# TensorE's program behind the experts put on both sides of the branch, and the compressed keys' product turned round and fed from split weight units

## What is computed

```python
chunks = kv.reshape(2, B, n_chunk, CMP_STRIDE, G, Dh)      # 16 tokens each
w1r = w1.reshape(2, r, CMP_STRIDE, Dh, CMP_HIDDEN)         # 2 x 2048 x 128 in all
pre = b1
for j in range(r):                                          # r = 2
    part = einsum('kbnpgd,kpdh->kbngh', chunks + pe, w1r[:, j])
    pre = pre + part[:, :, j:j + n_cmp]                     # n_cmp = 15
return einsum('kbcgh,khd->kbcgd', silu(pre), w2) + b2
```

## Time and profile before

| | us |
|---|---|
| median of 3 runs (lowest, highest) | 1060.5 (1059.07, 1060.95) |
| the profiled execution's own time | 1060.7 |
| span of its profile (first to last instruction) | 1058.7 |
| PE busy / PEld busy | 1012.6 / 844.4 |
| DVE busy / ACT busy | 734.1 / 609.1 |
| mean granted TensorE clock | 0.985 of full |

### The profile page before, as it was taken

How to read it: one execution, slowest core, us unless ns; L and a number is a source line. 1 busy time by engine, 2 the same in 40 slices (tenths; PEclk the granted TensorE clock), 3 DMA queues, 4 the chain that set the end, 5 groups by cost and what they waited for, 6 DMA issues and landing times.

```text
span 1058.7 us, 13638 instructions
## 1 busy us (share of the span) xinstructions
PE 1012.6 (96%) x5237; PEld 844.4 (80%) x5237; DVE 734.1 (69%) x813; ACT 609.1 (58%) x694; POOL 51.7 (5%) x47
## 2 busy tenths in 40 slices
PE   7999999997899999999799999999998898999998
PEld 6788788787788888877578888897877687888887
DVE  5534885678999999999955556566487755555664
ACT  6476433538899999988743443345375345344331
POOL 0011561011000000000000000000000000000000
PEclk9999999997999999999999999999899999999999
DMA  8923444452999999999946555873420044555511
GB/s 297 336 83 120 134 145 150 148 186 85 320 373 386 387 386 386 386 386 387 346 145 202 195 191 167 281 271 126 157 80 2 1 159 164 197 194 193 174 70 40
DMA packets 117021, 223.29 MB, mean 211 GB/s; under 512 B 6426, under 2 KB 12713, under 8 KB 116970
## 3 DMA queue, kind: packets, MB, share of 16 engines
q1 hardware_dynamic: 116426, 221.08, 60.2%
q0 software_dynamic: 384, 1.24, 0.3%
q10 hardware_dynamic: 160, 0.27, 0.1%
HBM read 221.49 MB, written 1.07 MB: 210 GB/s over the span
## 4 chain that ended last, share of the span: by engine, by line
PE 79%; DVE 8%; DMA 7%; ACT 4%; issue 2%; DVEq 0%; ACTq 0%; SPq 0%
PE ps L1830 18%; PE ps L1832 18%; PE ps L1831 18%; DMA w_raw<-in_w_exp_gate 6%; PE ps L2127 5%; PE ps L2128 5%; DVE w_lo L965 3%; ACT w_hi L537 2%; PE ps L2151 2%; PE ps L2168 1%; PE ps L2381 1%; PE ps L1996 1%; DMA w_raw<-in_w_exp_down 1%; PE ps L1876 1%; PE ps L1825 1%
## 5 line engine op out<-in xcount | busy, mean ns | idle before, releaser
L965 DVE TENSOR_TENSOR w_lo<-w_raw,w_hi 128x2048 fp32r<-128x2048 f32 x204 | 464.7, 2289 | 144.3 <-ACT w_hi L537 140.6
L537 ACT ACTIVATE w_hi<-w_raw 128x2048 fp32r<-128x2048 f32 x204 | 390.9, 1917 | 215.8 <-PE ps L1832 199.5
L1830 PE MATMUL ps<-w_hi,h_hi 128*128 128x512 f32 (+1 forms) x704 | 273.6, 389 | 9.7 <-DVE h_lo L992 6.7
L1831 PE MATMUL ps<-w_lo,h_hi 128*128 128x512 f32 (+1 forms) x704 | 268.8, 382 | 0.0
L1832 PE MATMUL ps<-w_hi,h_lo 128*128 128x512 f32 (+1 forms) x704 | 268.7, 382 | 0.0
L1830 PEld LDWEIGHTS ps<-w_hi,h_hi 128*128 128x128 f32 x704 | 133.3, 189 | 38.0 <-issue 11.7
L1832 PEld LDWEIGHTS ps<-w_hi,h_lo 128*128 128x128 f32 x704 | 133.2, 189 | 26.0
L1831 PEld LDWEIGHTS ps<-w_lo,h_hi 128*128 128x128 f32 x704 | 133.4, 189 | 23.8
L1830 PE MATMUL ps<-w_hi,aT_hi 128*128 128x512 f32 x176 | 68.9, 391 | 0.0
L1832 PE MATMUL ps<-w_hi,aT_lo 128*128 128x512 f32 x176 | 68.5, 389 | 0.0
L1831 PE MATMUL ps<-w_lo,aT_hi 128*128 128x512 f32 x176 | 68.5, 389 | 0.0
(11 more groups left out here) (354 smaller groups left out, 1276.3 us busy)
## 6 DMA issues: line engine op xcount, KB each, us to landing
w_raw<-in_ffn_w_in SPq DMA_DIRECT2D x44, 1024.0 KB, 5.1
w_raw<-in_w_exp_gate SPq DMA_DIRECT2D x32, 1024.0 KB, 10.7
w_raw<-in_w_exp_up SPq DMA_DIRECT2D x32, 1024.0 KB, 9.8
w_raw<-in_w_exp_down SPq DMA_DIRECT2D x32, 1024.0 KB, 10.8
w_raw<-in_w_in SPq DMA_DIRECT2D x22, 1024.0 KB, 7.8
w_raw<-in_ffn_w_out SPq DMA_DIRECT2D x22, 1024.0 KB, 5.0
w_raw<-in_w_mix_in SPq DMA_DIRECT2D x8, 1024.0 KB, 6.3
w_raw<-in_w_out SPq DMA_DIRECT2D x4, 1024.0 KB, 5.0
```

Source lines behind the costliest of these rows:

```text
L537: act.activation(w_hi[:, u % SPLIT, :], w_raw[:, u % RAW, :], ACT.Copy).then_inc(hi_ready, 1)
L965: dve.tensor_tensor(w_lo[:, u % SPLIT, :], w_raw[:, u % RAW, :], w_hi[:, u % SPLIT, :], ALU.subtract).then_inc(lo_ready, 1)
L1830: pe.matmul(out, hi, w_h, start=first, stop=False)
L1831: pe.matmul(out, hi, w_l, start=False, stop=False)
```

## The change

PE's program behind the experts becomes a function that is written once on each side of the branch (so on the few side no jump lies between the experts and the first FFN). The compression takes its weights from two more units of the common ring (8 of the 16 steps each, keys and values side by side), and the roles are turned: the columns of activations, hi and lo packed to 128, are the stationary side, and 256 weight columns move, once from `w_hi` and once from `w_lo`. A small product with `fold` sums the hi and lo rows. ACT and DVE make the packed hi and lo parts; the splits are reordered around the two new units. POOL loses one memset.

```diff
-U_MIXOUT = U_MIX + 8
+U_MIXOUT = U_MIX + 10
+U_CMP = (U_MIX + 5, U_MIX + 7)
+        kv_cmp = region_r("kv_cmp", 4096, PAIRS, 2, 2, 32)
+        def u_mix(i, kh):
+            return U_MIX + (0, 1, 2, 3, 4, 6, 8, 9)[2 * i + kh]
-        cmp_w1 = region(4096, 2, PAIRS, P)
-        kvT = region(13824, 2, 3, S)
+        cmp_sums = region(6144, 2, P)
+        def kv_src(g, odd):
+            v = ps[g * DH:(g + 1) * DH, 4, :].rearrange("p (k s) -> p k s", k=2)
+            return bass.AP(v.tensor, v.offset + odd, [list(v.ap[0]), list(v.ap[1]), [CMP_STRIDE, N_CMP], [2, PAIRS]])
+        def kv_of(low, g, odd):
+            v = kv_cmp[odd * DH:(odd + 1) * DH, :, low, :, N_CMP * g:N_CMP * (g + 1)]
+            return v.rearrange("p pp k c -> p k c pp")
...
 # SP
-            sp.dma_start(cmp_w1, a["cmp_w1_2"][0].rearrange("k (pp q) h -> q k pp h", q=P)).then_inc(cmp_in, 16)
-            for j in range(8):
-                mix_load(U_MIX + j)
+            def cmp_load(half):
+                u = U_CMP[half]
+                sp.wait_ge(lo_ready, u - RAW + 1)
+                dst = w_raw[:, u % RAW, :].rearrange("p (pp k h) -> p pp k h", k=2, h=P)
+                for kv, landed in enumerate((raw_in[u % RAW], cmp_in)):
+                    sp.dma_start(dst[:, :, kv], a["cmp_w1_2"][0, kv].rearrange(...)[:, 8 * half:8 * half + 8]).then_inc(landed, 16)
+            (mix_load of the units in order, cmp_load(0) behind (2, 0), cmp_load(1) behind (2, 1))
...
 # ACT
             leave_mix(0)
             split_hi(U_MIX + 4)
-            split_hi(U_MIX + 5)
+            act.wait_ge(cmp_in, 48)
+            split_hi(U_CMP[0])
+            act.wait_ge(kv_T, 1)
+            for g in range(2):
+                for odd in range(2):
+                    act.activation(kv_of(0, g, odd), kv_src(g, odd), ACT.Copy).then_inc(kv_hi, 1)
             leave_mix(1)
             split_hi(U_MIX + 6)
             head_rms(0, 16, 2)
-            split_hi(U_MIX + 7)
             act.wait_ge(gates_T, 2)
             (two sigmoids of the gates)
+            split_hi(U_CMP[1])
+            split_hi(U_MIX + 8)
+            leave_mix(2)
+            split_hi(U_MIX + 9)
             act.wait_ge(bias2_set, 1)
             (two silus to hidT)
-            leave_mix(2)
-            split_hi(U_MIX + 8)
+            split_hi(U_MIXOUT)
             head_rms(16, 24, 3)
-            split_hi(U_MIX + 9)
+            split_hi(U_MIXOUT + 1)
...
 # DVE
             sum_blocks(0)
+            (positions copied to kv_cmp, hi and lo, 4 small instructions)
-            split_lo(U_MIX + 5)
+            split_lo(U_CMP[0])
             dve.wait_ge(kv_T, 1)
             for g in range(2):
-                dve.tensor_copy(kvT[0:DH, :, g, :], src).then_inc(kvT_ready, 1)
-                dve.tensor_copy(kvT[DH:P, :, g, 0:S - 1], src[:, :, 1:S]).then_inc(kvT_ready, 1)
+                dve.wait_ge(kv_hi, 2 * g + 2)
+                for odd in range(2):
+                    dve.tensor_tensor(kv_of(1, g, odd), kv_src(g, odd), kv_of(0, g, odd), ALU.subtract).then_inc(kvT_ready, 1)
...
-            split_lo(U_MIX + 7)
+            split_lo(U_CMP[1])
             (nsink)
+            split_lo(U_MIX + 8)
+            dve.wait_ge(unit_used, U_CMP[1] + 1)
+            dve.tensor_copy(cmp_sums.rearrange("p k h -> p (k h)"), ps[:, 4, 0:2 * P]).then_inc(kvT_ready, 1)
+            sum_blocks(2)
             dve.wait_ge(pre_T, 1)
             (bias2)
-            split_lo(U_MIX + 8)
-            sum_blocks(2)
+            split_lo(U_MIX + 9)
             inv_rms(16, 24, 2)
             scale_keys(0, OFF_KA, 16)
             scale_heads(OFF_QB, 20, 4)
             scale_heads(OFF_QB + 256, 0, 4).then_inc(q_normed, 1)
+            split_lo(U_MIXOUT)
             dve.wait_ge(kvc_ready, 1)
...
-            split_lo(U_MIX + 9)
+            split_lo(U_MIXOUT + 1)
             k_out(0, 2, 5)
...
 # PE
             with pe.If(is_few > 0):
                 few_experts()
                 turn_sums()
+                behind_experts()
             with pe.Else():
                 (chunks, last_down, turn_sums)
+                behind_experts()
-            (the program from narrow to the last ffn, now the body of behind_experts)
...
+                def compress(half):
+                    pe.wait_ge(lo_ready, U_CMP[half] + 1)
+                    for n in range(PAIRS // 2):
+                        pp, wc = 8 * half + n, slice(2 * P * n, 2 * P * (n + 1))
+                        rows = kv_cmp[:, pp].rearrange("p l k c -> p (l k c)")
+                        pe.matmul(ps[:, 4, 0:2 * P], rows, w_hi[:, U_CMP[half] % SPLIT, wc], start=(pp == 0), stop=False)
+                        i = pe.matmul(ps[:, 4, 0:2 * P], rows, w_lo[:, U_CMP[half] % SPLIT, wc], start=False, stop=(pp == PAIRS - 1))
+                    i.then_inc(unit_used, 1)
+                def fold_sums():
+                    pe.wait_ge(kvT_ready, 9)
+                    for kv in range(2):
+                        i = pe.matmul(ps[:, 4, S + 64 * kv:S + 64 * kv + 32], cmp_sums[:, kv, :], fold[:, 32 * kv:32 * kv + 32], start=True, stop=True)
+                    i.then_inc(pre_T, 1)
-            pe.wait_ge(kvT_ready, 5)
-            (the 32 matmuls of L2341)
+                pe.wait_ge(kvT_ready, 8)
+                compress(0)
                 mix_unit(2, 1)
+                compress(1)
                 pe.wait_ge(mix_out, 4)
-            mix_unit(3, 0)
+                mix_unit(3, 0, inside=fold_sums, inside_at=1)
...
 # POOL
-            pool.memset(kvT[:, :, 2, :], 0.0).then_inc(pos_set, 1)
```

More of the change, by code:

```diff
@@ L502, in _, with mix_load @@
                 sp.dma_start(bias_t[:, n], bass.AP(bias_rows, n * HEADS * REL_W, [[1, P], [REL_W, HEADS], [1, S]])).then_inc(bias_in, 16)
-            def mix_load(u):
-                g, kh = MIX_ORDER[(u - U_MIX) // 2], (u - U_MIX) % 2
-                load(u, unit_src(a["w_mix_in_2"][0], 512 * kh, 512 * g))
-            for j in range(8):
-                mix_load(U_MIX + j)
+            def mix_load(i, kh):
+                load(u_mix(i, kh), unit_src(a["w_mix_in_2"][0], 512 * kh, 512 * MIX_ORDER[i]))
+            def cmp_load(half):
[3 more added lines that the diff above has]
+                for kv, landed in enumerate((raw_in[u % RAW], cmp_in)):
+                    sp.dma_start(dst[:, :, kv], a["cmp_w1_2"][0, kv].rearrange("(pp q) h -> q pp h", q=P)[:, 8 * half:8 * half + 8]
+                                 ).then_inc(landed, 16)
+            for i in range(2):
+                for kh in range(2):
+                    mix_load(i, kh)
+            mix_load(2, 0)
+            cmp_load(0)
+            mix_load(2, 1)
+            cmp_load(1)
+            mix_load(3, 0)
+            mix_load(3, 1)
             for kh in range(2):
@@ L2249, in _ @@
                 turn_sums()
[L2251 to L2257, removed]
-                        i = product(ps[:, banks[tt], 0:256], h_hi[:, k, c], h_lo[:, k, c], w_hi[:, u % SPLIT, wc],
-                                    w_lo[:, u % SPLIT, wc], k == 0, k == KT - 1)
-                i.then_inc(unit_used, 1)
@@ L2290, in _ @@
-            adds = ffn(U_FFN1, N_EXP, adds + 8, 13)
-            pe.wait_ge(tok_ready, 9)
-            transpose_cols(x, ident, (0, 1), ENTRY_BANKS)
-            def mix_second_half():
-                pe.wait_ge(tok_ready, 10)
-                transpose_cols(x, ident, (2, 3), ENTRY_BANKS)
-            def mix_unit(i, kh, rows=None, inside=None):
-                unit(U_MIX + 2 * i + kh, (2 * (i % 2), 2 * (i % 2) + 1), 4 * kh, kh == 0, kh == 1, rows=rows, inside=inside)
-            def transpose_q(c0):
-                for ct in range(4):
-                    for tt in range(TT):
-                        o = (ct % 2) * S + tt * P
-                        ins = pe.transpose(ps[:, 6 + ct // 2, o:o + P], proj[:, tt, c0 + ct * P:c0 + (ct + 1) * P], flip)
-                ins.then_inc(qk_T, 1)
@@ L2326, in _ @@
-            i.then_inc(kv_T, 1)
-            pe.wait_ge(wr_split_lo, 2)
-            for k in range(KT):
-                i = product(ps[0:GATE_COLS, 5, 0:S], wr_hi[:, k, :], wr_lo[:, k, :], h_hi[:, k, :], h_lo[:, k, :], k == 0, k == KT - 1)
-            i.then_inc(gates_T, 1)
-            pe.wait_ge(mix_out, 2)
-            mix_unit(2, 0)
-            pe.wait_ge(gateT_set, 1)
-            for tt in range(TT):
-                i = pe.transpose(ps[:, 5, S + 32 * tt:S + 32 * tt + GATE_COLS], gate_T[:, tt * P:(tt + 1) * P], ident[0:GATE_COLS, 0:GATE_COLS])
@@ L2336, in _ @@
-            i.then_inc(gates_T, 1)
-            pe.wait_ge(cmp_in, 32)
-            pe.wait_ge(kvT_ready, 5)
-            for kv in range(2):
-                for pp in range(PAIRS):
-                    i = pe.matmul(ps[:, 4, 64 * kv:64 * kv + 3 * N_CMP], cmp_w1[:, kv, pp, :],
-                                  kvT[:, kv, :, 2 * pp:2 * pp + CMP_STRIDE * (N_CMP - 1) + 1:CMP_STRIDE],
-                                  start=(pp == 0), stop=(pp == PAIRS - 1))
-            i.then_inc(pre_T, 1)
```

(1 more changed line is left out.)

399 lines of the change are left out of this document (220 added, 179 removed).

## The result

The median is **1052.8 us** over 11 runs (1048.9 to 1056.2); the kernel before had 1061.3 beside it. The ratio is 0.9909, 95% interval 0.9880 to 0.9937: faster by 0.9%, or 8.4 us, with 6.7 to 12.7 inside the interval. Forecast: 1050.4, range 1047.5 to 1056.0. The ratios in this document leave out two executions far outside all others, one of root_first (1681 us at a mean granted clock of 0.556) and one of the kernel before (1450 us at 0.65). The profiled execution took 1052.8, its span is 1050.6; before that was 1060.7 and 1058.7. So the trace has 8.1 us to account for.

The account below looks back on a forecast made before the run. PE was taken to bound the kernel, busy 96% of the span and 79% of the chain. The sum 1060.7 - 6.3 (join) - 4.8 (compression) + 1.0 (end) gave 1050.6, so a median of 1050.4 us, range 1047.5 to 1056.0.

Parts of the forecast that it names:

- The join, 4.6 + 1.7: Behind the branch: 4.6 us of PE waiting for a jump target's fetch and 1.7 of lower clock go, gain 6.3.
- Rival (a): At the join: the gap is the wait for DVE's h_lo that the timeline names, so it stays; 1055.7 us, chance 0.08.
- The end, a loss of 1.0: Few side's end: a new jump over the else side costs 1.0 us, the middle of bounds 0 and 1.9.
- the time above the span: Sign of being wrong: time exceeding the span by 4 us instead of 2 would mean the end jump at full price.
- The compression, 4.8: Mixing layer to start of attention: k_out at 777.2 instead of 782.06, gain 4.8 us, bounds 3.1 and 6.6.
- The wait of 1.1 us: Mixing layer: PE would wait 1.1 us for DVE's split of U_MIX + 6 if copies took the far bound, 1.2.
- DVE's wait for the root: Chain to attention: after its split at 766.4, DVE waits for ACT's root until 768.5.
- some 2 us: In front of the first logits: PE finishes its transposes at 776.1 and idles some 2 us until k_out at 777.2.
- Rival (b): Mixing layer gives nothing, as two more units of DVE and ACT work or a late copy eat the gain; 1055.2, chance 0.07.
- Attention and the last FFN shift as a whole.: Behind the mixing layer: both stages start earlier and keep their lengths, so no term is counted for them.
- The sum: Whole kernel: 1060.7 - 6.3 - 4.8 + 1.0 = 1050.6 for the profiled execution, 1050.4 for the median.
- Rival (c): FFN loops: moved code makes every round's jump back fetch, 38 us in all, so 1088; chance 0.04.

Follow-up runs that it names:

- root_first: The changed kernel with ACT's root for the keys' factors moved ahead of its copy of U_MIXOUT; 1054.6 us, ratio 0.9933.
- skip_long_again: Second execution of the changed kernel with a branch at the join jumping 320 never-run matmuls (640 instructions); 1061.3 us, ratio 1.000.
- the two shorter skips: The changed kernel with a branch at the join jumping 80 or 8 never-run matmuls (160 or 16 instructions); 1054.2 and 1054.5 us.
- compress_only: The changed kernel with the program behind the experts written once, behind the else side as before, so only the compression is new; 1058.5 us, ratio 0.9971.
- few_last: The changed kernel with PE's two sides exchanged, so the far jump lies at the branch's entry and none at the end; 1053.6 us, ratio 0.990.
- after_again: The changed kernel run once more with no edit; 1053.0 us, ratio 0.9920.
- the two halves: The duplicated program behind the experts alone, and the new compression alone, each against the kernel before; 1058.6 and 1058.5 us.
- join_only: The kernel before, with its program behind the experts on both sides of the branch and the old compression; 1058.6 us, ratio 0.9976.
- skip_long: First execution of the changed kernel with a branch at the join jumping 320 never-run matmuls; 3534 us, its 512-column matmuls at 1.1 us each.

## Why the prediction was right, and where it was off

The direction and the main mechanism held: 1050.4 forecast, 1052.8 and 1053.0 measured, inside the range. The gain was 8.4 us where 10.1 was forecast, and two terms of the sum were mis-sized.

- **The join, 4.6 + 1.7.** Measured 4.53 + 1.69. It was told from the code's first quarter of rows and one q8 packet, against the releaser that the timeline named. skip_long_again brings all of it back, and the two shorter skips nothing. Rival (a) falls.
- **The end, a loss of 1.0.** This term was mis-sized: it is 1.95, the upper bound (5.62 for 3.67; 1.7 to 2.0 over the profiles). The middle had been taken in case PE's queue ran ahead of the array. It does not hide the jump: compress_only and few_last, with no jump there, both end 3.7 us behind the last matmul. I had looked for it in the time above the span; it lies in the span (the time exceeds it by 2.2 us, before by 2.0).
- **The compression, 4.8.** Measured 4.38, in both traces and in compress_only. The 32 matmuls took 0.12 us each, as costed. The copies were taken at 0.6, though the nearest row has 0.68, so that "twice that" was 1.2; they took 1.04 and 1.09, close to this far bound. The wait of 1.1 us that was worked out for the bound came as 0.24, or 0.4 by the starts, and this is the term's miss: from the unit behind the wait to k_out the trace has 23.84 us and the prediction 23.8. DVE's wait for the root was predicted and came (2.07). The idling of "some 2 us" in front of the logits came as 1.30. Rival (b) falls.
- **"Attention and the last FFN shift as a whole."** The last FFN does, to 0.05 us. For attention the step is false for a single execution: 55.8 us in one profile of the changed kernel and 58.3 in the other. That is 2.3 us of the profiled execution's miss; against it stand 1.8 us by which the first stage was shorter. That these two nearly cancel is luck, since the prediction had neither.
- **The sum.** The terms that hang on the code give 6.22 + 4.38 - 1.95 = 8.65 us, where 10.1 was forecast; the medians say 8.4 (1061.3 - 1052.8), and after_again 7.9. The miss is the end (0.95) and the compression (0.4).
- **Rival (c)**: the changed kernel has 36 packets as before, none of them from 562 to 683, and the stretch of FFN to copy is shorter, not longer. It falls.

What stays open: the medians of the two halves alone give 2.4 and 2.5 us, the whole 8.4. The intervals (up to 5.2 and 5.1) allow the sum. In the profiles both halves had two falls in attention, and join_only a longer one at the old compression. Whether the halves make such falls likelier, or happened on them, these runs do not decide.

## What to carry to other kernels

If an engine stands still right behind the join of a branch, count what the jump skips and look for an instruction packet inside the gap, before believing the releaser that is named: a duplicated tail moved the jump to where it cost 1.95 us in place of 6.2. A far jump costs its full price, some 5.3 us here, less the work or the wait that lies over it, so compare the places where it could lie. And cut two traces at the same instructions into a table like the one above: the columns that repeat are the kernel's. Those that differ between executions of one kernel must not be put down to a change; here attention's differences go with the clock's falls.

## What the runs showed of the hardware

- PE's jump over 16 or 160 instructions that had not been run cost nothing that shows; over 640 it cost 4.65 us, and another 1.7 through the clock at its lower level behind it. A far jump left PE standing for 5.0 to 5.3 us at each of three places, whatever its length from 640 instructions up.
- The granted clock fell in attention in eight of the eleven profiles without fillers there (skip_long left out). Attention took 55.8 to 56.1 us without a fall and 57.5 to 60.9 with one or two; the same program had a fall in one execution and none in the next.
- The clock fell inside the 64 matmuls of 45 columns in both kernels that have them (one profile each), 4.7 and 5.4 us behind the first, with PE busy all the time. The 32 of 256 columns kept it full in all eleven profiles that have them.
- Copies and subtractions of 64 x 480 out of PSUM into the packed order took 1.04 us on ACT and 1.09 on DVE each, where DVE's 64 x 512 copy into plain order took 0.68.
